# A hybrid decoder layer on one core: early first-layer products for every fourth expert block, gathers one set ahead, last norms inside the expert stage

## The reference, cut to what matters

```python
h1 = layer_norm(ALPHA * x + mixed)
q = (h1 @ wq).reshape(n, heads=8, 2, 128)
s = einsum('nhcd,ckd->nhck', q, subkeys)           # two times 128 scores a head
sv, si = top_k(s, 16)
cand = sv[:, :, 0, :, None] + sv[:, :, 1, None, :]   # 16 x 16 sums
top_s, pos = top_k(cand, 16)                         # 16 experts a head, of 128 * 128
g = softmax(top_s)
hpre = einsum('nd,nhkd->nhk', h1, u_tab[eid])        # first layer of an expert: one row of u
f = einsum('nhk,nhkd->nd', gelu(hpre) * g, v_tab[eid])
y = layer_norm(ALPHA * h1 + f)
```

## Time and profile before

| what | value |
|---|---|
| median of 3 runs | 2648.16 us (2646.22 to 2648.57) |
| the profiled execution | 2648.93 us, its span 2647.1 us |
| PE, DVE, ACT, POOL busy | 87%, 61%, 35%, 14% of the span |
| mean clock granted to TensorE | 0.917 of full |
| DMA | 555.47 MB, mean 210 GB/s |

### The profile page before, as it was taken

How to read it: one execution, slowest core, us unless ns; L and a number is a source line. 1 busy time by engine, 2 the same in 40 slices (tenths; PEclk the granted TensorE clock), 3 DMA queues, 4 the chain that set the end, 5 groups by cost and what they waited for, 6 DMA issues and landing times.

```text
span 2647.1 us, 38437 instructions
## 1 busy us (share of the span) xinstructions
PE 2289.9 (87%) x13177; PEld 1955.8 (74%) x13177; DVE 1610.1 (61%) x3159; ACT 928.9 (35%) x1417; POOL 359.4 (14%) x370
## 2 busy tenths in 40 slices
PE   7997879998997989504376999999999999999994
PEld 7996656666664469503376999999999999999993
DVE  3433322343434347799994667777677776777767
ACT  3225533444445122102263333333333333333331
POOL 0000000000000000100000223222232222322230
PEclk9998879899988989856687999999999999999997
DMA  3220026667665111299965888888787887878873
GB/s 121 91 73 33 1 91 200 201 207 225 198 201 190 64 48 49 80 323 339 364 263 201 278 274 283 275 281 278 272 284 275 282 278 273 285 273 282 278 273 105
DMA packets 214837, 555.47 MB, mean 210 GB/s; under 512 B 16993, under 2 KB 87202, under 8 KB 212066
## 3 DMA queue, kind: packets, MB, share of 16 engines
q1 hardware_dynamic: 165730, 315.16, 36.3%
q0 software_dynamic: 49024, 239.23, 25.4%
HBM read 521.95 MB, written 98.83 MB: 235 GB/s over the span
## 4 chain that ended last, share of the span: by engine, by line
PE 68%; DVE 10%; DMA 5%; SPq 2%; ACT 2%; issue 1%; POOLq 0%; DVEq 0%; ACTq 0%; POOL 0%
PE psum L1913 20%; PE psum L1925 19%; PE psum L1523 4%; PE psum L1903 4%; DMA gates_dram<-gate_table 3%; PE psum L978 3%; PE psum L1386 3%; PE psum L1050 2%; PE psum L1032 2%; DVE gate_table L1726 2%; PE psum L968 2%; PE psum L1000 2%; DMA sample<-in_cache_v_sb_dram 2%; DVE gate_table L1723 1%; PE psum L1766 1%
## 5 line engine op out<-in xcount | busy, mean ns | idle before, releaser
L1913 PE MATMUL psum<-h_parts,expert_parts 128*128 128x384 f32 x3072 | 592.9, 341 | 4.2 <-DVE expert_parts L2013 4.2
L1925 PE MATMUL psum<-expert_parts 128*128 128x512 f32 x2304 | 557.2, 395 | 0.0
L1913 PEld LDWEIGHTS psum<-h_parts,expert_parts 128*128 128x128 f32 x3072 | 537.7, 189 | 14.6 <-DVE expert_parts L2013 4.8
L1925 PEld LDWEIGHTS psum<-expert_parts 128*128 128x128 f32 x2304 | 423.3, 188 | 83.5
L2013 DVE TENSOR_TENSOR expert_parts<-psum,expert_parts 128x512 fp32r<-128x512 f32 x256 | 177.1, 692 | 293.2 <-ACT expert_parts L1955 293.2
L1961 ACT ACTIVATE expert_parts<-peer 128x1024 fp32r<-128x1024 f32 x128 | 135.8, 1061 | 365.9 <-PE psum L1925 365.9
L1955 ACT ACTIVATE expert_parts<-psum 128x512 fp32r<-128x512 f32 x256 | 153.1, 598 | 200.5 <-PE psum L1903 200.5
L2053 DVE SCALAR_TENSOR_TENSOR kept<-experts,kept 128x1024 f32<-128x1024 f32 x160 | 204.7, 1280 | 3.9 <-DVE kept L2043 2.8
L1305 DVE TENSOR_TENSOR sample_parts<-sample,sample_parts 128x512 fp32r<-128x512 f32 x128 | 85.2, 690 | 158.0 <-ACT sample_parts L1158 158.0
L394 PE MATMUL psum<-projection_parts 128*128 128x256 f32 (+1 forms) x1440 | 173.7, 282 | 3.8 <-DVE projection_parts L500 3.8
L1883 POOL DMA_INDIRECT experts<-in_peer_u_dram,kept x96 | 113.0, 1178 | 468.5 <-DVE experts L2037 345.4
(11 more groups left out here) (271 smaller groups left out, 2993.7 us busy)
## 6 DMA issues: line engine op xcount, KB each, us to landing
peer<-in_peer_u_dram SPq DMA_DIRECT2D x128, 512.0 KB, 5.6
peer<-in_peer_v_dram SPq DMA_DIRECT2D x128, 512.0 KB, 3.7
sample<-in_cache_k_sb_dram SPq DMA_DIRECT2D x128, 256.0 KB, 3.1
sample<-in_cache_v_sb_dram SPq DMA_DIRECT2D x128, 256.0 KB, 3.0
out_dram<-in_state_k_win_dram POOLq DMA_DIRECT2D x8, 4088.0 KB, 104.9
out_dram<-in_state_v_win_dram POOLq DMA_DIRECT2D x8, 4088.0 KB, 118.2
gates_dram<-gate_table SPq DMA_DIRECT2D x12, 2048.0 KB, 8.4
experts<-gates_dram SPq DMA_DIRECT2D x32, 768.0 KB, 6.0
```

Source lines behind the costliest of these rows:

```text
L1913: last = pe.matmul(bank(6)[:, 0:ND], lhsT=u_t[s][:, a, k, :], rhs=h1_r[:, b, k, 0:ND], start=(k == 0 and n == 0), stop=(k == KD - 1 and n ...
L1925: last = pe.matmul(bank(2 * t + half), lhsT=weight[s][:, a, t * P:(t + 1) * P], rhs=v_r[s][:, b, half * 512:(half + 1) * 512], start=(firs ...
```

## The change

1. The 16 window copies are no longer issued in the gate stage but in four portions (`MOVES`): 7 in the stick-breaking stage, 4 at the start of the dilated stage, 3 of the norm stage, 2 of the query stage.
2. In the gate stage PE also makes the first layer of every fourth block (x = 4e + 3, 32 of them) from `h1_f`, h1 in fp32, with 8 fp32 products of 384 columns. ACT copies the turned u and takes gelu; the result (196 KB a block) goes to `gelu_dram`. Twelve blocks stand ahead of the turn of tile 0, five ahead of tile 1, five ahead of tile 2, and ten inside chunks 1 to 10. ACT's five exponentials stand in its queue behind blocks 1, 5, 10, 15 and 22. The table's copies use three pairs of banks in turn, not four.
3. In the expert stage these blocks skip u, its turn and `hidden`; their gelu is loaded a set ahead (`gelu_e`). The u buffers and their counts now run over the full blocks alone, so the u of the next set's first block is turned within the block k = 2 of a set.
4. Dots run one set ahead of the adds, and a set's adds stand within the set.
5. The last barrier is gone; the last `add_up` signals tile by tile, the last norms take tile 3 and the samples first, and the gains of the second norm are loaded in the first turn.
6. The query product is cut 384 + 256 in place of 320 + 320; ACT writes `h1_f` with six more copies.

```diff
+        MOVES = (7, 4, 3, 2)
+        def move_state(pool, turn):
+            for n in range(sum(MOVES[:turn]), sum(MOVES[:turn + 1])):
+                b = n // 2
+                to, frm = ((k_win_sample, state_k_win), (v_win_sample, state_v_win))[n % 2]
+                pool.dma_start(to[b]..., frm[b]...).then_inc(sem("window_moved"), 16)
...
+        EXP_AFTER = {1: 0, 5: 1, 10: 2, 15: 3, 22: 4}
+        BLOCK_OF = {1: 17, 2: 18, 3: 19, 4: 25, 5: 26, 6: 27, 7: 28, 8: 29, 9: 30, 10: 31}
+        FIRST_OF = ((0, 12), (12, 17), (20, 25))
+        def gate_schedule(turn, block, chunk):
+            for t in range(NTD + 1):
+                if t < NTD:
+                    for e in range(*FIRST_OF[t]):
+                        block(e)
+                    turn(t)
+                if t >= 1:
+                    for c in range(TILE_CHUNKS * (t - 1), TILE_CHUNKS * t):
+                        chunk(c, BLOCK_OF.get(c))
...
 (SP, gate stage)
+            def load(e):
+                if e < SETS:
+                    if e >= 2:
+                        sp.wait_ge(sem("early_turned"), 2 * e - 2)
+                    x = SET * e + SET - 1
+                    sp.dma_start(early_u[e % 2], peer_u[x * P:(x + 1) * P, :]...)
+            def block(e):
+                if e >= 1:
+                    store(e - 1)
+                load(e + 3)
...
 (PE, gate stage)
+            def hidden_early(e, half):
+                pe.wait_ge(sem("early_copied"), 2 * e + half + 1)
+                if half == 0 and e >= 1:
+                    pe.wait_ge(sem("early_gelu"), e)
+                for k in range(4 * half, 4 * half + 4):
+                    last = pe.matmul(bank(6)[:, 0:ND], lhsT=early_t[e % 2][:, k, :], rhs=h1_f[:, k, :], ...)
+            def block_half(e, half):
+                turn_early(e + 1, half)
+                hidden_early(e, half)
...
 (ACT, gate stage)
+            def block(e):
+                if e >= 1:
+                    gelu_early(e - 1)
+                copy_early(e + 1, 0)
+                copy_early(e + 1, 1)
+                exponents(e)
...
 (SP, expert stage)
                 for k in range(2 * SET):
                     x = 2 * SET * turn + k
+                    if k % SET == 0:
+                        if not (isinstance(turn, int) and turn == 0 and k == 0):
+                            sp.wait_ge(sem("weight_low"), x - 2)
+                        sp.dma_start(gelu_e[k // SET], gelu_dram[bass.ds(2 * turn + k // SET, 1)]...)
                     if not (isinstance(turn, int) and turn == 0 and k < 2):
-                        sp.wait_ge(sem("u_turned"), 2 * x + 2)
-                        sp.dma_start(u_sb[k % 2], peer_u[bass.ds(x * P, P), :])...
+                        if is_full(k):
+                            j = full_of(k)
+                            sp.wait_ge(sem("u_turned"), 2 * (FULL * turn + j) + 2)
+                            sp.dma_start(u_sb[j % 2], peer_u[bass.ds(x * P, P), :])...
                         sp.wait_ge(sem("v_low"), x + 1)
                         sp.dma_start(v_sb[k % 2], peer_v[bass.ds(x * P, P), :])...
...
 (PE, expert stage)
-                    for half in range(2):
-                        hidden(x, s, half)
-                        if not is_last(turn, k):
-                            turn_u(x + 1, 1 - s, SET * turn + (k + 1) // 2, half)
+                    if is_full(k):
+                        j = full_of(k)
+                        f = FULL * turn + j
+                        for half in range(2):
+                            hidden(f, j % 2, half)
+                            if not is_last(turn, k):
+                                turn_u(f + 1, 1 - j % 2, FULL // 2 * turn + (j + 1) // 2, half)
...
 (DVE, expert stage)
+                    if r in (1, 2) and not first:
+                        add(q, r + 1)
+                    gate(x, turn, k)
+                    if full:
+                        u_low(f + 1, 1 - e, 1)
+                    weight_low(x, s, k)
                     v_low(x, s)
+                    if r == (2 if first else 0):
+                        rows_gate(q)
+                        add(q, 0)
+                        add(q, 1)
...
+        LAST_ORDER = (NTD, NT - 1) + tuple(range(NTD))
```

More of the change, by code:

```diff
@@ L1778, in _ @@
+                    if e is not None:
+                        block_half(e, half)
+            turn_early(0, 0)
+            turn_early(0, 1)
+            gate_schedule(turn, block, chunk)
         @part("act")
         def _(act):
-            act.drain().then_inc(sem("table_copied"), 4)
+            act.drain().then_inc(sem("table_copied"), 3)
             act.drain().then_inc(sem("table_out_0"), 16)
             act.drain().then_inc(sem("table_out_1"), 16)
[L1784 to L1787, removed]
-                    act.activation(table[s][:, :, 8 * q:8 * q + 8].rearrange("p i n -> p n i"),
-                                   bank(2 * q, 2).rearrange("p (n i) -> p n i", n=8), ACT.Copy).then_inc(sem("table_copied"), 1)
@@ L1804, in build @@
+            copy_early(0, 0)
+            copy_early(0, 1)
+            gate_schedule(turn, block, chunk)
+            gelu_early(SETS - 1)
         for engine in programs:
@@ L1944, in _ @@
             over_turns(pe, blocks)
+            pe.wait_ge(sem("added"), PLACES * SETS)
+            pe.wait_ge(sem("gelu_done"), SETS * (SET - 1) + 2)
+            pe.wait_ge(sem("u_low"), 2 * SETS * (SET - 1) + 2)
+            for half in range(2):
+                last = pe.matmul(bank(6 + half)[0:NS, :], lhsT=pick, rhs=y_s[:, half * 512:(half + 1) * 512], start=True, stop=True)
+            last.then_inc(sem("f_turned"), 1)
             add_up(NK - 1, 1, final=True)
@@ L2008, in _, with weight_of @@
             dve.drain().then_inc(sem("gated"), 2 * SET)
+            def weight_of(k):
+                return gelu[full_of(k) % 2] if is_full(k) else gelu_e[k // SET]
             def u_low(x, s, half):
@@ L2062, in blocks @@
                     s, q, r = k % 2, 2 * turn + k // SET, k % SET
-                    before = not (isinstance(turn, int) and turn == 0 and k < SET)
-                    if not is_last(turn, k):
-                        u_low(x + 1, 1 - s, 0)
-                    if before and r >= 1:
-                        add(q - 1, r)
-                    gate(x, s, turn, k)
-                    if not is_last(turn, k):
-                        u_low(x + 1, 1 - s, 1)
-                    weight_low(x, s)
@@ L2090, in build @@
-        y_rows = y_prompt.rearrange("b (t p) d -> t (b p) d", p=P)
-        @part("pe")
-        def _(pe):
-            for half in range(2):
-                last = pe.matmul(bank(6 + half)[0:NS, :], lhsT=pick, rhs=y_s[:, half * 512:(half + 1) * 512], start=True, stop=True)
-            last.then_inc(sem("f_turned"), 1)
+                    first = isinstance(turn, int) and turn == 0 and k < SET
+                    final = isinstance(turn, int) and turn == SETS // 2 - 1 and k >= SET
+                    full = is_full(k) and not is_last(turn, k)
@@ new lines, in blocks @@
+                    if r == (2 if first else 0):
+                        rows_gate(q)
+                        add(q, 0)
+                        add(q, 1)
+                    if first and r == 3:
+                        add(q, 2)
+                        add(q, 3)
+                    if r == (2 if final else 3):
+                        add(q, 4)
+                    if not final:
+                        for p in ((), (), (0, 1), (2, 3, 4))[r] if first else ((0,), (1, 2), (3,), (4,))[r]:
+                            dot(q + 1, p)
```

290 lines of the change are left out of this document (188 added, 102 removed).

## The result

The median of 4 runs is 2691.95 us (2690.83 to 2695.68); the kernel before took 2648.36 beside it (2646.22 to 2653.4). The ratio is 1.0164, interval 1.0147 to 1.0182: slower by 43.6 us, where 49 us less had been forecast, and outside the range (2550 to 2640).

The account below looks back on a forecast made before the run. PE was taken to bound the expert stage and DVE the gate stage. Expert - 54, end - 26, gate + 16, norm + 13 and query + 2 sum to - 49 us: 2599 us, range 2550 to 2640.

Parts of the forecast that it names:

- 31 x (5.10 - 3.35) = 54 us are saved: Expert stage: each set saves 5.10 us of PE work, less a 3.35 us wait for u, over 31 sets.
- The wait: Expert stage, middle of each set's third block: PE waits 3.35 us for u, landing 5.1 us after issue; bounds 2.25 and 5.65.
- rival B: Expert stage: u(4) lands in 7.1 us, the wait is 5.35, the sets lose 8 us, total 2661 us; chance 0.09.
- the five extra dots of the first set meet a PE that starts slowly: Expert stage, first set: named under gathers, whose loads keep about three blocks of slack; given no size of its own.
- delay one u once, 2 us: Expert stage: gains of the second norm (1 MB) delay one u by 2 us, given back by start signals moved earlier.
- The end: Last set's start to the span's end: 86.5 us before, 60.6 after, saving 26 us (bounds 22 and 28).
- The gate stage: Gate stage: 17 us wait for the first exponential, 4 us chunk lag, less 5 of today's waits: + 16 us.
- rival C: Gate stage: PE bounds the chunks since its clock drops between blocks, + 25 us, total 2624 us; chance 0.14.
- moving them away wins nothing in that stage: Gate stage: window copies fill the DMA engines but hold nobody up; DVE's waits there come to 5.2 us.
- the 13: Norm stage: late gains behind three window copies cost + 13 us, taken as the middle, bounds 0 and + 25.
- Rival D: Norm stage: the gains of the norm land in time, - 13 us, total 2586 us; chance 0.20.
- if the queues take turns by packet: Norm stage: gains then land with the copies' end, 917 us, 17 us late; a slow clock adds 5 to 8.

Follow-up runs that it names:

- e1: Changed kernel with the u load of the next set's first block issued ahead of v of k = 3 and gelu_e in SP's queue: 2515.13 us, ratio 0.9492.
- e2: Changed kernel with 20 unused products of 384 columns on PE ahead of each late turn, load of u still late: 2647.69 us, ratio 0.9995.
- e5: Changed kernel with ACT's first exponential ahead of all blocks and the next three one block earlier each: 2694.12 us, ratio 1.0167.
- e6: Kernel before, with only its 16 window copies moved to the four portions of the change (7, 4, 3, 2): 2667.75 us, ratio 1.0070.
- e3: Changed kernel with the gelu_e load issued after v of its block, so u stands directly behind v(3): 2648.76 us, ratio 0.9992.
- e7: Changed kernel with u ahead of v in SP's queue, last window copies behind gains and weights, and first exponential first: 2495.56 us, ratio 0.9411.

## Why the prediction was wrong

**The step that failed** is "31 x (5.10 - 3.35) = 54 us are saved" in the expert stage. Its mechanism was right: the place (the middle of the third block), the cause (u behind an unrelated wait in SP's queue), and the issue in its size (+ 9.5 forecast, + 9.88 from the start of `hidden(1)` measured in the set shown). e1 shows that this one place decides 177 us. Two terms were off. The sums below are over the 29 steady sets; the first two come after.
- The wait: 4.0 us, not 3.35. The issue came some 0.4 us later than counted, and the load landed after 5.67 us (median of the 31 late ones; 4.67 to 10.21), where 5.1 was taken. That is 29 x 0.65 = 19 us.
- The clock: a term that was missing. The forecast had seen slow transposes behind idle PE, and charged them in the norm and gate stages, but not behind a wait of 3.35 us that it had itself put into every set. It measured 1.9 us a set, 29 x 1.9 = 55 us. e2 gets 44 us back: same late load, products in the gap, and products at full speed behind it in nearly every set. It can't give back all, since its own products (3.5 us) and the 1.0 us of wait that is left (25.7 over 26 times) come to more than the gap of 4.0.

With both, a set gives back more than the 5.10 us it saves (4.0 + 1.9 = 5.9), and the sign turns. The forecast had called the landing time its weakest point, at 31 us for each us. But its own wait, with the clock charged, would already have left nothing: the seven steady sets of the trace whose wait was 3.06 to 3.53 us took 36.7 us on average, the 36.8 of before. The bounds of the wait (2.25 to 5.65) held 4.0, but the price of a us of waiting didn't hold: rival B, 5.35 us of wait and 2661 us, is nearest to what came, but the wait that it asks for did not come, and its nearness is luck.

**The first two sets** cost 13.3 us more than before (4.8 + 8.5). The forecast's "the five extra dots of the first set meet a PE that starts slowly" and "delay one u once, 2 us" were both too cheap: the first u is late by 7.86 us, and the second set has, beside its late turn, 1.17 us of wait for the u behind the gains and 4.53 for DVE, with slow products behind that one. How the 8.5 us share out between the gains and DVE's delay was not tested. These 13, with the 19 and the 55 above, are the distance between - 54 and + 32.9.

**The end**: - 17.2, not - 26. The length after the change was right (60.6 forecast, 60.1 measured). The length of before was mis-read: the `hidden` at 2588.1 was taken for that of the last block and is that of the one before it; from the start of the last set to the end of the span it was 77.3 us and not 86.5. The 9.2 us are this mistake, and they alone take a fifth of the forecast gain.

**The gate stage**: + 11.5, + 16 forecast. The wait for the first exponential was 12.7 (17, or 12 if the clock comes early), the lag in the chunks 4.1 (4), and 6.59 us a half on PE (6.6). The accounting holds; its reading as two waits that could be removed one by one doesn't: e5 takes the first away and finds PE behind it. So rival C was right that PE is the bound in the chunks, and wrong in its reason: the granted clock is 0.97 from 1247 to 1300 and 1.00 from 1300 to 1440.

**The copies**: "moving them away wins nothing in that stage" was off by the 4.7 us of waits that e6 no longer shows, though the forecast's own sum took 5 us off for them. In the norm stage + 9.5 (13 forecast) and in the query stage + 4 (2, at most 8): right in size, but the 13 was the middle between two cases and not worked out from either. The gain landed at 904.0, 0.15 us before the second of the three copies (in e6 at 913.55, 0.17 before the second). Rival D, gains in time, was false: by bytes they would have been there at 888. The packets from 878 to 890 and from 890 to 904 (packets, MB, share) are:

```profile
q0 software_dynamic: 77, 4.06, 90.8%
q1 hardware_dynamic: 79, 0.32, 8.2%
```
```profile
q0 software_dynamic: 83, 4.32, 88.5%
q1 hardware_dynamic: 81, 0.21, 8.8%
```

The copies (queue q0) and the loads (q1) have almost the same count of packets served, while the copies' packets hold 53 and 52 KB and those of the loads 4.1 and 2.6. So the forecast's case "if the queues take turns by packet" is what the trace shows. The Trainium skill ("DMA: Bandwidth & Descriptors", Queues, rings and completion order) has each DMA engine take turns between queues by the packet; the trace agrees, with 77 against 79 and 83 against 81. That the forecast's working by it, 901 us, is near the 904.0 does not confirm the working: it took "only one or two turns", and 160 packets of copies, ten for each of 16 engines, went through between 878 and 904. A small load with many small packets beside a copy in large ones waits nearly as long as the copy does.

## What to carry to other kernels

- When loads for a later step are issued in program order on one queue, write down for each load the time at which its buffer is free, the time at which its turn in the queue comes, and the time at which it is wanted; when an edit takes work out between the last two, the order of the queue has to be made anew. Here one issue moved by one place was worth 177 us of 2692.
- A gap in PE has two prices, the gap and the slow products that can stand behind it; look in the trace of before for a gap of that length and read the next products, and charge both in a loop. With waits of 4.0 us on average the second price came in 30 of 31 sets, with 3.0 us (e3) in 16 of 31.
- After a wait has been found, ask what would have come due right behind it: e5 took 8 us from one wait, 7 came back in the next, and the time stayed.

## What the runs showed of the hardware

- After a PE wait of 4.84 us, four transposes took 1.11 us in place of 0.44 and twelve products 3.00 in place of 2.11; the granted clock was 0.50 in the transposes. After a wait of 2.71 us in e3 they took 0.65 and 2.09. The same product can thus be slow or fast in neighbouring sets.
- Products whose result is thrown away made the kernel 44 us faster (e2), since they stood in the gap.
- The DMA engines moved 312 to 315 GB/s with a share of 0.90 to 0.92 beside a PE that was busy 947 of 950 us (e1) and 932 of 940 (e7): the 0.81 and 278 GB/s of before were not their limit.
- The two gains of the first norm, 512 KB each, were issued 0.4 us apart, at 873.18 and 873.57, and the first of three copies of 4 MB at 873.45. The first gain landed after 4.3 us, the second after 30.4, where it took 5.3 before.
- From 878 to 904 the queue of the copies and that of the loads had 160 packets each served, of 8.38 and of 0.53 MB.
